# A two-layer decoder trunk on one core: which engine makes the low parts of the weights, and three smaller edits

## The chip, the cores and the metric

The kernel runs on one core of one Trainium2 chip. The metric is the device time of one execution in microseconds, as the median of several runs. TensorE (PE in the profile) multiplies, VectorE (DVE), ScalarE (ACT) and GpSimd (POOL) compute elementwise, SyncE (SP) issues most of the transfers.

## The reference

The input is one sequence of 256 tokens with 1024 features, all in float32. With `rms(x, g)` for x / sqrt(mean(x²) + 1e-6) · g:

```python
# layer 0
x = x + mlstm_layer(x, ...)      # rms -> q, k, v, o, gates; matrix memory in 4 heads; @ w_out
x = x + conv_ffn(x, layer 0)     # rms -> @ w_up (1024 x 5632), causal convolution of width 3,
                                 # silu(gate) * val, @ w_down (2816 x 1024)
# layer 1
k_sh, v_sh = rms(x, kv_norm_g) @ w_kv            # 3 dilation groups x 16 heads x 64
q = rms(x, b_norm_g) @ b_w_q
x = x + merge(dilated attention of 3 groups, relative bias) @ b_w_out
x = x + conv_ffn(x, layer 1)
return rms(x, final_norm_g)
```

## The kernel before

Features lie on the partitions: X is 128 x 8 x 256 (feature block k, token). Every weight matrix is read in **units** of 1024 x 256 float32 (1 MB), 124 in all, one after the other: 0 to 11 for the mLSTM's projections, 12 to 15 for its output, 16 to 37 for the first FFN up, 38 to 49 down, 50 to 85 for Q, K and V, 86 to 89 for the attention's output, 90 to 111 and 112 to 123 for the second FFN. Unit n lives in **slot** n % 3 of a ring of three (RING): `raw[s]` as loaded by SyncE's queue, `whi[s]` its high part, `wlo[s]` the low part. ScalarE makes the high part (`hi`, L487: a copy to fp32r). The low part is raw - whi, in `lo`: on VectorE (L832) two instructions of 128 x 1024, on GpSimd (L448) four of 128 x 512. Before the change VectorE does slot 0 and GpSimd slots 1 and 2 (unit 1 is shared). TensorE does three matmuls for each pair of k and column half: high · high, high · low (L1284, L1285), low · high (L1286). Activations are split likewise into `xsA`, `xsB`, `hs`, `aTs`.

Each engine runs its own hand-written order. `hi(n)` waits for the load and for TensorE to have used unit n - 3 (`w_used`). `lo(n)` waits for `hi_done`, TensorE for `lo_done` (in two halves), and the load of unit n + 3 for `lo_done` as well. Everything that stands behind a wait in an engine's order waits too.

- **mLSTM** (units 0 to 11). In pass u VectorE first calls `lo(u + 2)` and then does the work of gates and heads: `head_done` (L930 max, L933 reciprocal, L936 product), `head_normed` (L944, L946), and in pass 11 `gated` for k = 0 to 3 (L872) and `m_lo` (L878), on which the output projection waits.
- **Output projections** (`outproj`). VectorE adds each tile to X (`residual`, L897), ScalarE scales the new X (`gained`, L495) and squares it, VectorE makes the low part of the scaled X (`gained`, L848) and sums the squares (L857).
- **FFN up** (`ffn`, `pair`). A pair is two units, four tiles j in banks FB = (2, 3, 0, 1). VectorE scales a tile by rstd (`scaled`, L1069), ScalarE makes the first tap (`first_tap`, L664), VectorE the two others (`taps`, L1075 and L1079), and TensorE may use the bank again when the last tap is done (`cB_done`). VectorE calls `lo(n + 2)` at the start of the pair and `lo(n + 3)` behind the taps of tile 0. In the first pair `rstd_of` (L883, a reciprocal) is behind `lo(n + 2)`.
- **Attention** (`block`, four of them with nine units each). Tiles of Q, K and V are evacuated by `evac` (L1244, L1249, L1252); scores go into banks 3 to 5, a reduction with the bias gives the row maxima (L1169), ScalarE takes exp (L727) and normalises (L735), TensorE transposes (`turned`, L1551), ScalarE and VectorE split the transposed P (`p_hi` L751, `p_lo` L1187), and `mixed` multiplies P by V (L1570) into banks PV_BANK = (5, 4). In `mixed(0)` TensorE waits for `smax_done` of all eight score tiles, as scores use bank 5. In the last block the tiles of the output projection's first unit (`projected`) are interleaved with this.
- **End.** The sum of squares of the last norm (L1629, L1631), root (L519), reciprocal (L883). Then VectorE makes Y = X · gain · rstd for k = 0 to 4 (L1274), while GpSimd multiplies the three others, which ScalarE has scaled (L816), by rstd (L472). Four stores follow.

## Time and profile before

| | |
|---|---|
| median of 3 runs | 805.54 us (804.18 to 806.45) |
| the profiled execution | 804.01 us |
| its span, first to last instruction | 802.0 us |
| mean granted TensorE clock | 0.988 |
| TensorE busy | 768.8 us, 96% of the span |
| VectorE busy | 469.2 us |
| ScalarE busy | 458.9 us |
| GpSimd busy | 432.3 us |

Times in the trace are microseconds from the first instruction. The profiled execution is one of its own, 2 us longer than its span. A busy TensorE is not a TensorE at its peak, since matmuls overlap; the count of matmuls in a stretch and the granted clock tell more.

### The profile page before, as it was taken

What the parts mean: (1) busy time and instruction counts of PE and PEld (TensorE: products, weight loads), DVE (VectorE), ACT (ScalarE), POOL (GpSimd) and SP (SyncE); (2) the same over time, 40 slices, a digit from 0 to 9 for tenths busy, and PEclk for the clock granted to TensorE, in tenths of its full rate; (3) what the DMA queues carried; (4) which work ended last, traced back from release to release, by engine and by line L of the source; (5) the groups of instructions that cost most, each with busy time, mean ns of one, the idle gap of its engine ahead of it and who ended that gap; (6) DMA issues with size and microseconds to landing.
All of it is one profiled execution on the core that took longest, in us unless ns stands there. A gap on an engine that the chain in (4) does not pass through costs nothing.

```text
span 802.0 us, 17242 instructions
## 1 busy us (share of the span) xinstructions
PE 768.8 (96%) x6550; PEld 753.5 (94%) x6550; DVE 469.2 (58%) x905; ACT 458.9 (57%) x603; POOL 432.3 (54%) x346
## 2 busy tenths in 40 slices
PE   7999989999999999989999999999899999999994
PEld 6989989999999999989999999999899999999994
DVE  5766858767677344446435544635557767676333
ACT  6543547665666456358647737746756665665441
POOL 2843446666556667652563554452255666556851
PEclk9999989999999999999999999999999999999997
DMA  9634425646565456864676486476415756554721
GB/s 293 199 114 149 159 94 169 206 163 209 185 198 181 158 188 200 226 225 94 177 228 144 143 210 143 145 209 186 117 53 161 248 171 207 180 194 138 232 96 52
DMA packets 135612, 137.26 MB, mean 171 GB/s; under 512 B 3521, under 2 KB 134932, under 8 KB 135572
## 3 DMA queue, kind: packets, MB, share of 16 engines
q1 hardware_dynamic: 127808, 130.03, 49.8%
q10 hardware_dynamic: 7764, 6.67, 6.4%
q8 instruction: 28, 0.46, 0.2%
q14 instruction: 12, 0.10, 0.0%
HBM read 135.57 MB, written 1.12 MB: 170 GB/s over the span
## 4 chain that ended last, share of the span: by engine, by line
PE 77%; DVE 10%; ACT 5%; issue 4%; DMA 3%; DVEq 0%; ACTq 0%; SPq 0%
PE bank L1284 12%; PE bank L1286 12%; PE bank L1285 12%; PE banks L1284 8%; PE banks L1286 8%; PE banks L1285 8%; PE bank L1504 3%; PE banks L1570 3%; PE bank L1506 3%; PE bank L1505 3%; PE banks L1536 2%; PE banks L1551 2%; DVE wlo L832 2%; DMA raw<-in_w_kv 2%; ACT whi L487 2%
## 5 line engine op out<-in xcount | busy, mean ns | idle before, releaser
L448 POOL TENSOR_TENSOR wlo<-raw,whi 128x512 fp32r<-128x512 f32 (+1 forms) x325 | 423.4, 1337 | 335.0 <-ACT whi L487 334.8
L487 ACT ACTIVATE whi<-raw 128x2048 fp32r<-128x2048 f32 (+1 forms) x136 | 238.0, 1751 | 206.7 <-PE bank L1286 97.4
L1284 PE MATMUL bank<-xsA,whi 128*128 128x256 f32 x568 | 158.7, 279 | 6.7 <-DVE wlo L907 3.0
L1286 PE MATMUL bank<-xsA,wlo 128*128 128x256 f32 x568 | 157.0, 276 | 0.0
L1285 PE MATMUL bank<-xsA,whi 128*128 128x256 f32 x568 | 156.9, 276 | 0.0
L1284 PE MATMUL bank<-xsB,whi 128*128 128x256 f32 x480 | 134.3, 280 | 0.8 <-DVE X L897 0.3
L1286 PE MATMUL bank<-xsB,wlo 128*128 128x256 f32 x480 | 132.7, 276 | 0.0
L1285 PE MATMUL bank<-xsB,whi 128*128 128x256 f32 x480 | 132.6, 276 | 0.0
L832 DVE TENSOR_TENSOR wlo<-raw,whi 128x1024 fp32r<-128x1024 f32 x83 | 106.2, 1316 | 18.7 <-ACT whi L487 18.2
L1284 PEld LDWEIGHTS bank<-xsA,whi 128*128 128x128 f32 x568 | 106.6, 188 | 8.2 <-issue 3.8
L1285 PEld LDWEIGHTS bank<-xsA,whi 128*128 128x128 f32 x568 | 106.7, 188 | 0.1
L1286 PEld LDWEIGHTS bank<-xsA,wlo 128*128 128x128 f32 x568 | 106.6, 188 | 0.0
L1284 PE MATMUL banks<-hs,whi 128*128 128x256 f32 x352 | 97.2, 276 | 0.0
L1285 PE MATMUL banks<-hs,whi 128*128 128x256 f32 x352 | 97.2, 276 | 0.0
L1286 PE MATMUL banks<-hs,wlo 128*128 128x256 f32 x352 | 97.2, 276 | 0.0
L1284 PEld LDWEIGHTS bank<-xsB,whi 128*128 128x128 f32 x480 | 90.1, 188 | 2.8 <-DVE Vs L1252 1.0
L1285 PEld LDWEIGHTS bank<-xsB,whi 128*128 128x128 f32 x480 | 90.2, 188 | 0.0
L1286 PEld LDWEIGHTS bank<-xsB,wlo 128*128 128x128 f32 x480 | 90.1, 188 | 0.0
L1284 PEld LDWEIGHTS banks<-hs,whi 128*128 128x128 f32 x352 | 66.1, 188 | 0.0
L1285 PEld LDWEIGHTS banks<-hs,whi 128*128 128x128 f32 x352 | 66.1, 188 | 0.0
L1286 PEld LDWEIGHTS banks<-hs,wlo 128*128 128x128 f32 x352 | 66.1, 188 | 0.0
L1075 DVE SCALAR_TENSOR_TENSOR cb<-bank,vcols,cb 128x255 f32<-128x255 f32 x66 | 31.6, 479 | 51.4 <-ACT cb L664 51.2
(200 smaller groups left out, 1630.4 us busy)
## 6 DMA issues: line engine op xcount, KB each, us to landing
raw<-in_f_w_up SPq DMA_DIRECT2D x44, 1024.0 KB, 5.1
raw<-in_w_kv SPq DMA_DIRECT2D x24, 1024.0 KB, 5.4
raw<-in_f_w_down SPq DMA_DIRECT2D x16, 1024.0 KB, 5.2
raw<-in_b_w_q SPq DMA_DIRECT2D x12, 1024.0 KB, 5.2
raw<-in_a_w_in SPq DMA_DIRECT2D x10, 1024.0 KB, 5.6
raw<-in_f_w_down SPq DMA_DIRECT2D x8, 768.0 KB, 4.9
Bi<-bias_by_distance ACTq DMA_DIRECT2D x16, 384.0 KB, 6.2
raw<-in_a_w_out SPq DMA_DIRECT2D x4, 1024.0 KB, 5.3
```

The costliest lines, as they stand in the source:

```text
L448: o = g.tensor_tensor(wlo[s][:, ka:kb, :], raw[s][:, ka * CW:kb * CW] .rearrange("p (k c) -> p k c", c=CW), whi[s][:, ka:kb, :].bitcast(F3 ...
L487: o = a.activation(whi[s][:, k0:k1, :], raw[s][:, k0 * CW:k1 * CW] .rearrange("p (k c) -> p k c", c=CW), ACT.Copy)
L832: v.tensor_tensor(wlo[0][:, ka:kb, :], raw[0][:, ka * CW:kb * CW].rearrange("p (k c) -> p k c", c=CW), whi[0][:, ka:kb, :].bitcast(F32), A ...
L1075: v.scalar_tensor_tensor(cb[:, j, 1:S], bank[FB[j]][:, 0:S - 1], conv_col(layer, 1, p * 2 + (KF * g + c)), cb[:, j, 1:S], ALU.mult, ALU.ad ...
L1284: t_.matmul(ps, hi_w, hi_x, start=first, stop=False)
L1285: t_.matmul(ps, hi_w, lo_x, start=False, stop=False)
L1286: return t_.matmul(ps, lo_w, hi_x, start=False, stop=last)
L1504: t_.matmul(ps, xs[:, k, 0, cs], whi[s][:, k, :], start=first, stop=False)
L1505: t_.matmul(ps, xs[:, k, 0, cs], wlo[s][:, k, :], start=False, stop=False)
L1506: mm = t_.matmul(ps, xs[:, k, 1, cs], whi[s][:, k, :], start=False, stop=last)
L1536: mm = t_.matmul(score_out(2 * t + j)[:, g * w:(g + 1) * w], QT[rows, g, hp, tt * P:(tt + 1) * P], KT[rows, g, hp, 0:w], start=True, stop= ...
L1570: mm = t_.matmul(pv_out(h, slice(0, P))[:, kt * P:S], w, x[:, h, g, 2 * kt:2 + kt, :].rearrange("p b q -> p (b q)"), start=g == kt == 0 an ...
```

## The change

1. VectorE makes the low parts of slots 0 and 1, GpSimd those of slot 2 and of unit 18 (POOL_UNIT). In GpSimd's order: the rest of unit 1, then 2, 5, 8, 11, 14, 17, 18, 20, 23 and so on.
2. In the first FFN pair `rstd_of` comes before `lo(n + 2)`. In the attention block `evac(j, 0)` comes before `lo(n0 + j + 2)`; `lo(n0 + 9)` is called before `evac(8, 0)`; in the output projection `lo(u0 + 5)` is called in pass 2.
3. In the last block P times V of heads 0 and 1 goes to bank 2 instead of bank 5. `mixed(0)` then has no wait for `smax_done`, and the output projection waits for the low parts of these heads (`alo_done`) before its second unit, which uses bank 2.
4. For k = 0 to 4 of the last norm ScalarE writes X · gain into PSUM (`final_gained`, banks 0 to 2) during the last columns, and VectorE multiplies it by rstd with a tensor_tensor.

```diff
+POOL_UNIT = U_UP0 + 2
-PV_BANK = (5, 4)
+PV_BANK = ((5, 4), (2, 4))
...
-            return bank[PV_BANK[h // 2]][rows, (h % 2) * S:(h % 2 + 1) * S]
+            return bank[PV_BANK[last][h // 2]][rows, (h % 2) * S:(h % 2 + 1) * S]
...
+        def final_gained(k):
+
+            return bank[k // 2][:, k % 2 * S:(k % 2 + 1) * S]
# GpSimd
-            for n in range(U_IN, 6):
-                if n % RING:
-                    lo(n, k0=SHARE if n == 1 else 0)
+            lo(1, k0=SHARE)
+            lo(2)
+            lo(5)
...
-            with pool.Fori(0, (U_END - 7) // RING) as i:
-                for n in (7, 8):
-                    lo(n, i, RING)
+            with pool.Fori(0, (POOL_UNIT - 8) // RING + 1) as i:
+                lo(8, i, RING)
+            lo(POOL_UNIT)
+            with pool.Fori(0, (U_END - POOL_UNIT) // RING) as i:
+                lo(POOL_UNIT + 2, i, RING)
# ScalarE, ffn
                 warm_root()
+                if not sets:
+                    for k in range(Y_POOL):
+                        act.wait_ge(x_new, q0 + k + (1 - KD))
+                        a.activation(final_gained(k), X[:, k, :], ACT.Copy, scale=col(V_FIN + k))\
+                            .then_inc(yx_done, 1)
# VectorE, lo
-                if n % RING or n >= U_END:
+                s = n % RING
+                if s == 2 or n >= U_END or n == POOL_UNIT:
                     return
-                dve.wait_ge(hi_done[0], rnd(n, i, step) + 1)
+                dve.wait_ge(hi_done[s], rnd(n, i, step) + 1)
...
# VectorE, outproj
                     if u == 1:
                         lo(u0 + 3)
                         lo(u0 + 4)
+                    if u == 2:
+                        lo(u0 + 5)
# VectorE, pair
-                    lo(n + 2, i, step)
                     if first:
                         rstd_of(s, S)
+                    lo(n + 2, i, step)
                     scaled(p, 0, n, i, step)
# VectorE, block
                 for j in range(4):
+                    evac(j, 0)
                     lo(n0 + j + 2, i, step)
-                    evac(j, 0)
                     evac(j, 1)
...
                 a_lo(0)
                 a_lo(1)
+                lo(n0 + 9, i, step)
                 evac(8, 0)
# VectorE, end
+            dve.wait_ge(yx_done, Y_POOL)
             for k in range(Y_POOL):
-                v.scalar_tensor_tensor(Y[:, k, :], X[:, k, :], col(V_FIN + k), rstd[:, 0:S],
-                                       ALU.mult, ALU.mult).then_inc(yn_done, 1)
+                v.tensor_tensor(Y[:, k, :], final_gained(k), rstd[:, 0:S], ALU.mult)\
+                    .then_inc(yn_done, 1)
# TensorE, outproj
                 pe.wait_ge(ev_done, e0)
+                if begun:
+                    pe.wait_ge(alo_done, HB * (NHB - 1) + 2)
# TensorE, mixed
-                        pe.wait_ge(smax_done, hb * 8 + 8)
+                        if not last:
+                            pe.wait_ge(smax_done, hb * 8 + 8)
```

## Rows read from the trace of the kernel before

**Rows 1.** The page's first part: busy time, share, instructions of each engine.
```profile
PE 768.8 (96%) x6550; PEld 753.5 (94%) x6550; DVE 469.2 (58%) x905; ACT 458.9 (57%) x603; POOL 432.3 (54%) x346
```

**Rows 2.** Windows: stretch, its length, busy time and (instructions), clock, DMA share, GB/s.
```profile
105.00:110.00 5.00, 4.92 (x23) 4.95 (x24) 4.83 (x13) 2.85 (x8) 0.00 (x0) 0.50 0.63 210
351.00:356.00 5.00, 4.76 (x45) 4.64 (x46) 2.36 (x11) 2.70 (x7) 4.38 (x4) 1.00 1.04 340
575.00:578.00 3.00, 3.00 (x15) 3.00 (x16) 1.05 (x1) 0.98 (x2) 0.00 (x0) 0.50 0.20 49
160.00:260.00 100.00, 100.00 (x883) 100.00 (x883) 71.31 (x141) 61.43 (x74) 62.66 (x51) 1.00 0.58 189
```

**Rows 3.** Waits of TensorE: us in total, times, longest.
```profile
PE banks L1284 <- DVE xsB L878: 3.6, 1, 3.6
...
PE banks L1570 <- DVE mxx L1169: 2.4, 1, 2.4
PE banks L1536 <- DVE KT L1249: 2.3, 1, 2.3
```

**Rows 4.** L832: ns min/median/max; timeline of VectorE in the second output projection.
```profile
L832 DVE TENSOR_TENSOR wlo<-raw,whi x83: 1210/1219/2316, 11.6 to 779.2; 128x1024 fp32r<-128x1024 f32 x83
...
602.89 1.51 DVE L848 SCALAR_TENSOR_TENSOR xsB<-X,vcols,xsB 128x256 fp32r<-128x256 f32 x1
...
610.55 0.48 DVE L848 SCALAR_TENSOR_TENSOR xsB<-X,vcols,xsB 128x256 fp32r<-128x256 f32 x1 [0.32 <-ACT xsB L495]
```

**Rows 5.** Timeline of VectorE in the mLSTM: start us, us, instructions, [idle before].
```profile
75.73 1.35 DVE L930 TENSOR_TENSOR den<-den,EB 128x256 f32<-128x256 f32 x1 [2.38 <-ACT den L607]
...
98.46 1.50 DVE L946 TENSOR_TENSOR hm<-hm,hrs 128x512 f32<-128x512 f32 x1
...
100.22 4.38 DVE L872 SCALAR_TENSOR_TENSOR hm<-hm,vcols,sig 128x256 f32<-128x256 f32 x4
...
106.53 0.86 DVE L872 SCALAR_TENSOR_TENSOR hm<-hm,vcols,sig 128x256 f32<-128x256 f32 x2
```

**Rows 6.** Timeline of VectorE and ScalarE before the first FFN pair.
```profile
138.24 2.36 DVE L832 TENSOR_TENSOR wlo<-raw,whi 128x1024 fp32r<-128x1024 f32 x2 [1.88 <-ACT whi L487]
...
138.04 0.46 ACT L519 ACTIVATE rstd<-banks,epsc 128x256 f32<-128x256 f32 x1
```

**Rows 7.** Timeline of VectorE and ScalarE in the first attention block.
```profile
346.25 4.27 DVE L832 TENSOR_TENSOR wlo<-raw,whi 128x1024 fp32r<-128x1024 f32 x2 [3.74 <-ACT whi L487]
...
344.30 1.92 ACT L487 ACTIVATE whi<-raw 128x2048 fp32r<-128x2048 f32 x1 [0.96 <-DMA raw<-in_w_kv]
```

**Rows 8.** Timeline of TensorE and ScalarE in the last attention block.
```profile
574.88 0.48 PE L1570 MATMUL banks<-PTh,Vs 128*128 128x256 f32 x1 [2.44 <-DVE mxx L1169]
...
574.03 0.92 ACT L735 ACTIVATE SB<-SB,linv 128x768 f32<-128x768 f32 x1
...
581.08 0.94 ACT L735 ACTIVATE SB<-SB,linv 128x768 f32<-128x768 f32 x1
```

**Rows 9.** Timeline in the FFN pairs of layer 0; last, a wait in 160 to 268.
```profile
190.29 0.48 DVE L1079 SCALAR_TENSOR_TENSOR cb<-banks,vcols,cb 128x254 f32<-128x254 f32 x1
...
190.88 0.33 PE L1284 MATMUL banks<-xsA,whi 128*128 128x256 f32 x1
...
204.80 1.92 ACT L487 ACTIVATE whi<-raw 128x2048 fp32r<-128x2048 f32 x1 [2.10 <-PE banks L1286]
...
207.64 0.47 DVE L1075 SCALAR_TENSOR_TENSOR cb<-bank,vcols,cb 128x255 f32<-128x255 f32 x1
...
DVE cb L1075 <- ACT cb L664: 22.2, 12, 2.0
```

**Rows 10.** Timeline of VectorE, SyncE's queue and ScalarE at the end.
```profile
794.38 3.56 DVE L1274 SCALAR_TENSOR_TENSOR Y<-X,vcols,rstd 128x256 f32<-128x256 f32 x5
...
796.31 3.01 SPq L415 DMA_DIRECT2D out<-Y  x4
...
788.46 0.39 ACT L500 ACTIVATE banks<-X 128x256 f32<-128x256 f32 x1 [8.88 <-DVE X L897]
```

More of the change, by code:

```diff
@@ L269, in build @@
         ahi_done, alo_done = sem("ahi_done"), sem("alo_done")
-        yg_done = sem("yg_done")
+        yg_done, yx_done = sem("yg_done"), sem("yx_done")
         yn_done, yp_done = sem("yn_done"), sem("yp_done")
@@ L299, in own_rows, with pv_out, head_out @@
             return slice((h % 2) * DH, (h % 2 + 1) * DH)
-        def pv_out(h, rows):
-            return bank[PV_BANK[h // 2]][rows, (h % 2) * S:(h % 2 + 1) * S]
-        def head_out(hb, h, part):
+        def pv_out(h, rows, last):
+            return bank[PV_BANK[last][h // 2]][rows, (h % 2) * S:(h % 2 + 1) * S]
+        def head_out(hb, h, part, last):
             rows = own_rows(h)
@@ L310, in head_out @@
                 .rearrange("p a (b t) -> p (a b) t", b=NT)
-            src = pv_out(h, rows).rearrange("p (b t) -> p b t", b=NT)[:, :, ::-1]
+            src = pv_out(h, rows, last).rearrange("p (b t) -> p b t", b=NT)[:, :, ::-1]
             return dst, src
@@ L760, in a_cross @@
                         act.wait_ge(asum_done, hb * HB + (h - 1))
-                    a.activation(cross[own_rows(h), :], pv_out(h, own_rows(h + 1)), ACT.Copy)\
+                    a.activation(cross[own_rows(h), :], pv_out(h, own_rows(h + 1), last), ACT.Copy)\
                         .then_inc(cross_done, 1)
@@ L766, in a_hi @@
                     act.wait_ge(asum_done, hb * HB + (h + 1))
-                    a.activation(*head_out(hb, h, 0), ACT.Copy).then_inc(ahi_done, 1)
+                    a.activation(*head_out(hb, h, 0, last), ACT.Copy).then_inc(ahi_done, 1)
                 act.wait_ge(bv_out, 16)
@@ L825, in lo @@
             def lo(n, i=0, step=0, k0=0, k1=KD):
-                if n % RING or n >= U_END:
+                s = n % RING
+                if s == 2 or n >= U_END or n == POOL_UNIT:
                     return
-                dve.wait_ge(hi_done[0], rnd(n, i, step) + 1)
+                dve.wait_ge(hi_done[s], rnd(n, i, step) + 1)
                 for ka in range(k0, k1, KD // 2):
                     kb = ka + KD // 2
-                    v.tensor_tensor(wlo[0][:, ka:kb, :],
-                                    raw[0][:, ka * CW:kb * CW].rearrange("p (k c) -> p k c", c=CW),
-                                    whi[0][:, ka:kb, :].bitcast(F32), ALU.subtract)\
-                        .then_inc(lo_done[0], 1 if n else 2)
+                    v.tensor_tensor(wlo[s][:, ka:kb, :],
+                                    raw[s][:, ka * CW:kb * CW].rearrange("p (k c) -> p k c", c=CW),
+                                    whi[s][:, ka:kb, :].bitcast(F32), ALU.subtract)\
+                        .then_inc(lo_done[s], 1 if n else 2)
             def acc_clear(q):
@@ L1195, in a_sum @@
                     dve.wait_ge(cross_done, hb * HB + (h // 2 * 2 + 2))
-                    ps = pv_out(h, own_rows(h))
+                    ps = pv_out(h, own_rows(h), last)
                     v.tensor_tensor(ps, ps, cross[own_rows(h), :], ALU.add).then_inc(asum_done, 1)
@@ L1201, in a_lo @@
                     dve.wait_ge(ahi_done, hb * HB + (h + 1))
-                    dst, src = head_out(hb, h, 1)
-                    v.tensor_tensor(dst, src, head_out(hb, h, 0)[0].bitcast(F32), ALU.subtract)\
+                    dst, src = head_out(hb, h, 1, last)
+                    v.tensor_tensor(dst, src, head_out(hb, h, 0, last)[0].bitcast(F32), ALU.subtract)\
                         .then_inc(alo_done, 1)
                 for j in range(4):
+                    evac(j, 0)
                     lo(n0 + j + 2, i, step)
-                    evac(j, 0)
                     evac(j, 1)
@@ L1570, in mixed @@
                                     mm = t_.matmul(
-                                        pv_out(h, slice(0, P))[:, kt * P:S], w,
+                                        pv_out(h, slice(0, P), last)[:, kt * P:S], w,
                                         x[:, h, g, 2 * kt:2 + kt, :].rearrange("p b q -> p (b q)"),
```

## The prediction

> **What bounds the kernel now.** I read the page first: TensorE is busy for 96% of the span, VectorE for 58%, GpSimd for 54% [rows 1]. So no engine but TensorE can be worth more than TensorE's idle time. The table of windows shows that in the long FFN stretch TensorE runs 883 matmuls in 100 us with no idle time at the full 2.4 GHz [rows 2]; less work on GpSimd gains nothing there. The gain has to come from the few stalls between stages, so the waits of TensorE come next: 3.6 us for the low parts of the mLSTM output (L878), 2.4 us for the row maxima (L1169) in the last attention block, 2.3 us for a K tile (L1249) at the first block [rows 3]. After the longest two TensorE also runs at 1.2 GHz for a while, and after the 2.3 us stall it does not [rows 2]. Outside TensorE there is the tail after its last matmul. I then followed the timeline around each of these.
>
> **Who does the low parts.** There are 124 weight units. VectorE now splits the 41 whole ones of slot 0 (83 instructions of 1.22 us, L832, with one half [rows 4]). Afterwards GpSimd has slot 2 and unit 18, VectorE the rest of slots 0 and 1: 161 instructions, 39 units more on balance. A unit is two instructions of 1.22 us, 2.3 to 2.4 us; that is some 90 us more on VectorE and about 200 us less on GpSimd. Alone this is neither gain nor loss. What counts is where the 2.35 us lands, and what happens when both engines work at once: a scalar_tensor_tensor on operands in SBUF takes 0.48 us with GpSimd idle and 1.51 us while GpSimd subtracts [rows 4]. By the Trainium skill ("SBUF — State Buffer", Who interferes with whom) a VectorE instruction with two SBUF inputs contends with a GpSimd instruction that reads SBUF, and one of them waits for all of the other; these rows agree. The change takes most such overlaps away. The steps, in order of time:
>
> **mLSTM, to 105 us.** The chain here runs over VectorE. It now holds the splits of units 4, 7, 10 and 13. Unit 4 falls into slack. Unit 7 waits for ScalarE's copy and delays the gate exponents, estimated 0.3 us on TensorE. Unit 10 (2.35 us) cannot begin before 75.5 and precedes den at 75.73; den loses its contention (1.35 to 0.43 us) [rows 5]: about 1.1 us late. Unit 13 comes before the four hm products: 2.35 us added, but those four took 4.38 us against 0.86 for two without GpSimd [rows 5], so 2.7 us come back, and 0.8 us on L946 (1.50, of which I put 0.7 to its work). Sum 0.3 + 1.1 + 2.35 - 2.7 - 0.8: 0.3 us late. Bounds: 1 us gained to 2 lost. I take 0.4 lost. TensorE reaches this stall about 1.4 us later, so it idles about 2.5 us instead of 3.6. Whether the clock then falls I can't tell: idle 2.3 us it stayed up, idle 2.4 us (before L1570) it fell. The low clock cost 23 matmuls in 5 us where 44 fit [rows 2], about 2.5 us with its end. I take the fall as likelier.
>
> **First FFN pair, both layers.** In layer 0 the reciprocal of the root now precedes the split that sat in front of it (2.36 us at 138.24 [rows 6]), and that split goes to GpSimd; but the root is ready only at 138.5 [rows 6], and VectorE then gets unit 19 between the taps of the first tile and those of the second, while GpSimd is on unit 18. Of 2 us saved I keep 0.5 (0 to 2).
>
> **First attention block.** The K tile waits because the split of unit 57 (4.27 us, contended, begun at 346.25 when ScalarE had copied a slab that landed at 344.3) precedes both of its evacuations [rows 7]. Now the first of them goes ahead, and the other still waits for the split. The load of that slab is issued after unit 54's split as before; earlier loads go out 2 us sooner, but the bias loads hold the DMA engines then. If nothing but the first evacuation moves it gains 0.3 us, if the slab comes 2 us sooner all 2.3. I take 0.9. In the steady blocks the moved splits fit between softmax steps; two weight loads are issued together just before the bias loads, which may cost up to 2 us in one block: I take 0.2 lost.
>
> **Last attention block.** P times V of heads 0 and 1 starts at 574.88 after 2.44 us of idle time, because scores lie in bank 5 until their maxima are taken [rows 8]. With bank 2, whose last V tile VectorE has read before, it begins at 572.3 at full clock. The 16 matmuls before the transposes (some 3.4 us at the low clock, 15 in 3 us [rows 2]) then take 1.8; the transposes need ScalarE's normed P of 574.03 + 0.92 [rows 8], so TensorE idles 0.9 us. The next transposes need the copy at 581.08 [rows 8], which hangs on the former by way of p_hi, p_lo and inverse: it comes at 577.9, and all behind it by 3.2 us earlier. The new wait on alo_done stands before matmuls that TensorE reaches 2 us after it is met. Gain 3.2 us (2.0 if the transposes' chain takes 1.2 us back; 3.7 with the stall and the slow clock wholly gone).
>
> **Second output projection and its FFN pair.** The split of unit 91 leaves GpSimd for VectorE. The four STTs beside it took up to 1.51 us, and take 0.48 without it [rows 4]: some 3.3 us for the four, of which the new split takes 2.3 and waits for ScalarE 0.3. Net 0.7 us (0 to 1.5).
>
> **FFN pairs, 22 of them.** Three pairs last 32.6 us; VectorE is busy for 71.31% [rows 2], 23.3 us. Two more splits make 28.0. So it holds on average. But order matters: in a pair with a split behind its first taps, the second taps end at 190.77 and TensorE overwrites that bank at 190.88, with 0.33 us for a matmul that else lasts 0.28 [rows 9]: no slack. Where the preceding pair ended in a split, the first taps start 0.33 us later than they can (207.64, after 204.80 for the copy, against 2.51 us elsewhere [rows 9]). In the new pattern of slots these two meet every third pair, six times in both layers: 6 x 0.33, and with the smaller ones 2.0 us lost (0.5 to 5).
>
> **Tail.** Five STTs on X and rstd, both in SBUF, take 3.56 us beside GpSimd's three [rows 10]. With gained X in PSUM each has one SBUF input. At the pace of the pair that takes 0.86 us [rows 5] five take 2.0; a tensor_tensor is a little shorter, so I take 1.8. ScalarE's five copies come after the last table load, in 8.88 us in which it only waits for X [rows 10], and cost nothing; without that cover they would take 2 us. The four stores, issued over 3.01 us from 796.31 [rows 10], follow. Gain 1.8 us (1.2 to 2.2).
>
> **Sum.** Against the profiled execution's 804.01 us (span 802.0): gains 0.5 + 0.9 + 3.2 + 0.7 + 1.8 = 7.1; losses 0.4 + 0.2 + 2.0 = 2.6; net 4.5 us, 799.5. That execution lies 1.5 us under the median, 805.54; so 801.0 us.
>
> **Rivals.**
> 1. *The clock stays up at 105 us*, or the FFN pairs lose nothing. Each is worth 2 to 2.5 us: 798.5, with both 796.5. For it: 2.3 us idle left the clock alone [rows 2, 3]. Against it: 2.44 us brought it down in the last block [rows 2, 8].
> 2. *The move pays for itself and no more.* The FFN loss reaches its bound of 5 us and the last block gives 2: net 0.3, 805.2. That is no change.
> 3. *Slower: VectorE can't fill its waits in the FFN pairs.* Besides its busy time it waits 22.2 us in ten pairs for ScalarE's first tap (L664) [rows 9], 6.7 in three pairs. If no split fits into those, 28.0 + 6.7 = 34.7 us against 32.6: 2.1 us in each three pairs, 15 us in all, net 8.5 slower, 814. It is decided at 1.2 us for each three pairs (8.9 in all): above that the kernel is over 2.4 us slower. Against it: behind a split the first taps start 2.84 us after the copy, 0.33 late [rows 9], so that the split has filled the wait but for this. What would bring it about is contention: a split beside GpSimd took 4.27 us instead of 2.35 [rows 4, 7], and two such in three pairs add 3.8 us. VectorE's splits begin 3.6 and 9.0 us after the copy of a pair, when GpSimd, which starts as soon as its own slab is copied and needs 5.1 us, is done with slot 2 or has not begun, so I don't expect it. The Trainium skill ("Perfetto Trace Analysis", Optimizing Scalar/DVE Operations) says that moving work between these two engines might not help, as they share a port; the rows that bear it out are those of the contended split.
>
> **Chances.** Forecast, 799 to 803: 0.50. Rival 1, 796 to 799: 0.27. Rival 2, 803 to 808: 0.15. Rival 3: 0.08. The measurement can tell 0.3%, 2.4 us. Faster than 803.1: 0.79; within: 0.14; slower than 808: 0.07. Both ends of the range, 796.5 and 804.3, take in rival 1 and half of rival 2.
>
> **What would show it.** L832 x161, L448 x169, the latter never beside L872. L1570's first start in the last block within 0.3 us of the matmul before, at full clock. The five products at the end within 2 us. Waits of TensorE for L1079 in every third pair, 0.3 us each; if they are 1.2 us or in every pair, rival 3. At the first block the wait for L1249 shorter than 2.0 us. The granted clock between 104 and 111 us tells rival 1. The prediction fails if the FFN stretch runs under 870 matmuls in 100 us, or if the last block's chain gives less than 2 us.

## The result, and the profile after

The changed kernel takes 797.8 us in the median (795.02 to 799.05, five runs) and the kernel before 804.18 us (803.63 to 806.45) beside it. By the medians that is 6.4 us faster. The ratio of the two is put at 0.9899, 95% interval 0.9881 to 0.9917, which is 8.1 us (6.7 to 9.6); the same pair measured again (experiment 5) gives 7.1 us by the medians and 7.2 by the ratio. The profiled execution took 795.02 us with a span of 793.0, 9.0 us under the span of before. One of all the runs in this document, in experiment 4, was a slow one of 865.7 us at a mean granted clock of 0.843; the ratio and the range there leave it out. Three parts of the prediction's sum came out to 0.1 us, and the total still fell short of the measured change, so the places matter more than the total.

The page's first part and two of its groups. GpSimd has 190 instructions instead of 346 [rows 1], VectorE 161 instructions of its split, two to a unit, instead of 83 [rows 4].

```profile
PE 767.4 (97%) x6550; PEld 751.1 (95%) x6550; DVE 538.5 (68%) x983; ACT 462.4 (58%) x608; POOL 226.7 (29%) x190
...
L453 POOL TENSOR_TENSOR wlo<-raw,whi 128x512 fp32r<-128x512 f32 (+1 forms) x169 | 218.2, 1324 | 530.4 <-ACT whi L494 530.4
...
L845 DVE TENSOR_TENSOR wlo<-raw,whi 128x1024 fp32r<-128x1024 f32 x161 | 197.9, 1267 | 15.8 <-ACT whi L494 15.1
```

Waits of TensorE in the changed kernel, to be held against [rows 3]: the mLSTM's wait (xsB, L891) has shrunk from 3.6 to 2.3 us, and those for the row maxima and for KT are gone. Of the seven waits for cb (L1094) in the first line two are old: 1.24 and 1.18 us in the first pair of either layer, where before waited 1.49 and 1.22. The other five, 0.15 to 0.16 us each, are new, and a sixth is too short for the list.

```profile
PE banks L1301 <- DVE cb L1094: 3.2, 7, 1.2
PE banks L1301 <- DVE xsB L891: 2.3, 1, 2.3
...
PE banks L1570 <- ACT SB L747: 1.3, 2, 0.7
...
PE banks L1590 <- DVE PTl L1202: 0.5, 1, 0.5
```

Windows of the changed kernel (columns as in [rows 2]): behind the mLSTM's stall, in the FFN pairs of either layer, and the P times V of the last block. Where before ran 23 matmuls at a clock of 0.50 this execution runs 42 at 1.00; the FFN pairs have lost their full house, 872 and 869 matmuls where 883 and 881 fitted; and nothing in the last block is at the low clock.

```profile
105.00:110.00 5.00, 5.00 (x42) 4.85 (x43) 4.82 (x14) 2.98 (x7) 0.00 (x0) 1.00 0.48 169
155.00:255.00 100.00, 99.54 (x872) 98.95 (x871) 83.76 (x153) 62.10 (x74) 30.35 (x24) 1.00 0.59 190
...
632.00:732.00 100.00, 99.53 (x869) 98.85 (x868) 82.76 (x150) 60.91 (x72) 30.35 (x24) 1.00 0.55 183
...
568.00:571.00 3.00, 2.29 (x21) 2.15 (x20) 2.62 (x8) 3.00 (x6) 0.00 (x0) 1.00 0.00 2
```

The two traces have the same 6550 matmuls, so the plainest comparison is when a matmul of a given number starts in each. The table is that start minus the start in before's profiled execution; two executions of the changed kernel, the split alone (experiment 1) and before with the end alone (experiment 3) stand side by side. The last runs before's code up to the last matmuls, so that it shows how far before's own profiled execution can be taken as usual.

| behind (matmul, its time in before) | changed, 793.0 us | changed again, 795.3 us | split alone, 799.2 us | end alone, 800.6 us | predicted |
|---|---|---|---|---|---|
| mLSTM's stall and clock (760, 111.5) | -2.6 | -1.2 | -1.25 | -1.15 | +0.4 |
| first FFN pair (1060, 149.3) | -3.5 | -1.2 | -1.2 | -1.2 | -0.1 |
| FFN pairs of layer 0 (2700, 336.0) | -2.2 | +0.1 | 0.0 | -1.3 | +0.9 |
| first attention block (3300, 407.7) | -4.5 | -2.15 | -2.3 | +0.4 | 0.0 |
| the other blocks (4600, 558.1) | -4.5 | -2.1 | -1.8 | +0.4 | +0.2 |
| last block (4740, 578.8) | -7.7 | -5.3 | -3.3 | +0.5 | -3.0 |
| second output projection (5000, 611.6) | -8.5 | -6.1 | -4.1 | +0.5 | -3.7 |
| FFN pairs of layer 1 (5860, 712.0) | -7.15 | -4.9 | -2.8 | +0.4 | -2.7 |
| end | -9.0 | -6.7 | -2.85 | -1.4 | -4.5 |

Read the second column against the first: the same kernel, 2.3 us apart, all of it gained before matmul 1060 and nothing after. The experiments below had to say what that is. And read the fourth column by itself: before's code, run again, is 1.2 us ahead of before's profiled execution behind the mLSTM and loses 1.7 us against it in the first block. Experiments 2 and 4 do the like (2.5 and 1.2 us ahead, then 2.1 and 1.95 lost), and this changes what the stages of the change are worth.

### The profile page after: what moved, and what is told of

The parts are those of the page before. It is cut to its first block, busy times and chain, and to the rows that moved or that the text cites. A ratio compares the mean times of both kernels' runs of the same rounds, so it can differ in the third digit from the quotient of the medians.

```text
span 793.0 us, 17171 instructions
## 1 busy us (share of the span) xinstructions
PE 767.4 (97%) x6550; PEld 751.1 (95%) x6550; DVE 538.5 (68%) x983; ACT 462.4 (58%) x608; POOL 226.7 (29%) x190
## 4 chain that ended last, share of the span: by engine, by line
PE 53%; DVE 24%; issue 11%; ACT 7%; DMA 2%; DVEq 1%; ACTq 0%; POOL 0%; POOLq 0%
DVE wlo L845 9%; PE bank L1301 7%; PE bank L1303 6%; PE bank L1302 6%; PE banks L1301 6%; PE banks L1303 6%; PE banks L1302 6%; DVE cb L1090 3%; PE bank L1523 3%; PE banks L1590 2%; PE bank L1525 2%; DVE bank L1084 2%; ACT cb L671 2%; PE bank L1524 2%; PE banks L1555 2%
## 5 line engine op out<-in xcount | busy, mean ns | idle before, releaser
L453 POOL TENSOR_TENSOR wlo<-raw,whi 128x512 fp32r<-128x512 f32 (+1 forms) x169 | 218.2, 1324 | 530.4 <-ACT whi L494 530.4
L845 DVE TENSOR_TENSOR wlo<-raw,whi 128x1024 fp32r<-128x1024 f32 x161 | 197.9, 1267 | 15.8 <-ACT whi L494 15.1
L1523 PE MATMUL bank<-whi,xsA 128*128 128x256 f32 x192 | 56.8, 296 | 0.0
```

What stands on the lines that cost most here:

```text
L453: o = g.tensor_tensor(wlo[s][:, ka:kb, :], raw[s][:, ka * CW:kb * CW] .rearrange("p (k c) -> p k c", c=CW), whi[s][:, ka:kb, :].bitcast(F3 ...
L845: v.tensor_tensor(wlo[s][:, ka:kb, :], raw[s][:, ka * CW:kb * CW].rearrange("p (k c) -> p k c", c=CW), whi[s][:, ka:kb, :].bitcast(F32), A ...
L1523: t_.matmul(ps, xs[:, k, 0, cs], whi[s][:, k, :], start=first, stop=False)
```

## The experiments

Each group of experiments has runs of before beside it: 804.93 us median for the first four, 804.49 for the next four, 805.03 for 9 to 11 and 804.58 for 12. Differences are of medians within a group, where nothing else is said.

**1. The split alone.** The changed kernel without its points 3 and 4:

```diff
-PV_BANK = ((5, 4), (2, 4))
+PV_BANK = ((5, 4), (5, 4))
...
-                        if not last:
-                            pe.wait_ge(smax_done, hb * 8 + 8)
+                        pe.wait_ge(smax_done, hb * 8 + 8)
...
-            dve.wait_ge(yx_done, Y_POOL)
...
-                v.tensor_tensor(Y[:, k, :], final_gained(k), rstd[:, 0:S], ALU.mult)\
-                    .then_inc(yn_done, 1)
+                v.scalar_tensor_tensor(Y[:, k, :], X[:, k, :], col(V_FIN + k), rstd[:, 0:S],
+                                       ALU.mult, ALU.mult).then_inc(yn_done, 1)
```

> The changed kernel with the old banks for P times V and the old end: only the move of slot 1's low parts to VectorE and the new places of the splits. My theory: the move alone gains 3.5 to 4 us in the profiled execution: 2.7 by 105 us if the clock stays at 2.4 GHz there (0.2 if it falls), 0.5 in the first FFN pair, 2.3 in the first attention block, 0.7 in the second output projection, less 2.6 in the FFN pairs (six waits for L1094's counterpart of 0.3 us, and smaller ones). The rival, that the move only pays for itself and the gain is all in the bank and the end, expects a total within 1 us of the kernel before.

802.33 us (800.4 to 805.11), ratio 0.9974 [0.996, 0.9987]: 2.6 us faster, the span 2.85 shorter, with the clock fallen at 105 us. That is neither the theory's 3.5 to 4 nor the rival's "within 1 us". The wait for KT is gone with this part alone, and the 2.44 us for the maxima stand. The table shows 1.5 us gained in the last block all the same: behind that unchanged stall the clock was 1.00 (39 matmuls from 575 to 580 us), in before's execution 0.66 (31). It fell in experiments 3, 4 and 9 as well, so this part of the gain is not shown to be the split's.

**2. Bank 2 alone** (before with point 3) and **3. the end alone** (before with point 4):

```diff
# 2
-PV_BANK = (5, 4)
+PV_BANK = ((5, 4), (2, 4))
...
+                if begun:
+                    pe.wait_ge(alo_done, HB * (NHB - 1) + 2)
...
-                        pe.wait_ge(smax_done, hb * 8 + 8)
+                        if not last:
+                            pe.wait_ge(smax_done, hb * 8 + 8)
# 3, with ScalarE's five products of point 4
...
+            dve.wait_ge(yx_done, Y_POOL)
             for k in range(Y_POOL):
-                v.scalar_tensor_tensor(Y[:, k, :], X[:, k, :], col(V_FIN + k), rstd[:, 0:S],
-                                       ALU.mult, ALU.mult).then_inc(yn_done, 1)
+                v.tensor_tensor(Y[:, k, :], final_gained(k), rstd[:, 0:S], ALU.mult)\
+                    .then_inc(yn_done, 1)
```

> The kernel before with bank 2 for P times V of heads 0 and 1 in the last block, its wait for the maxima gone and the new wait in the output projection; nothing else. My theory: 3.2 us faster, TensorE's 2.4 us wait before L1570's line gone, no stretch at 1.2 GHz near 575 us, and a wait of 0.7 to 0.9 us for the transposes in its place. The rival, that the chain of transposes takes it back, expects 2.0 us or less.

> The kernel before with the gained X of the last norm in PSUM; nothing else. My theory: VectorE's five products take 1.8 us instead of 3.56, and the span is 1.8 us shorter from the last matmul on. The rival, that the stores or GpSimd's three products decide the end, expects under 0.5 us. ScalarE's five copies should start within the stretch in which it waits for X, and no other wait should grow.

Bank 2: 801.29 us, ratio 0.996 [0.9947, 0.9973]. Between matmuls 4600 and 4740 its trace gains 3.25 us, the predicted 3.2. In the place of the wait for L1169 stands the one that the prediction had named, ScalarE's normed P, and it is short. TensorE's timeline there, and then VectorE's at the end of the kernel with the end alone:

```profile
574.50 0.88 PE L1560 MATMUL banks<-ident,SB 128*128 128x128 f32 x6 [0.78 <-ACT SB L740]
```
```profile
794.83 1.75 DVE L1287 TENSOR_TENSOR Y<-bank,rstd 128x256 f32<-128x256 f32 x5
```

The end: 802.28 us, ratio 0.9972 [0.996, 0.9984]; behind the last matmul its trace gains 1.8 us, five products in 1.75 us instead of 3.56 [rows 10].

Both kernels run before's code up to the first attention block, and both lose there what before's profiled execution did not. The wait for KT is 3.0 and 2.5 us instead of 2.3, and behind it the clock falls, while in [rows 2] it stood at 1.00 with 45 matmuls in 5 us. Against before, experiment 2 loses 2.1 us between matmuls 2700 and 3300 and experiment 3 loses 1.7. Windows of 2 and of 3, then their waits:

```profile
350.00:355.00 5.00, 5.00 (x39) 4.78 (x38) 2.17 (x10) 2.29 (x6) 3.44 (x3) 0.75 1.09 363
```
```profile
350.00:355.00 5.00, 4.84 (x32) 4.62 (x33) 2.02 (x11) 1.44 (x4) 4.27 (x4) 0.66 1.05 347
```
```profile
PE banks L1545 <- DVE KT L1256: 3.0, 1, 3.0
```
```profile
PE banks L1549 <- DVE KT L1261: 2.5, 1, 2.5
```

**4. The order alone** (before with the two moves of point 2: the root ahead of the split, the first evacuation ahead of the split).

```diff
-                    lo(n + 2, i, step)
                     if first:
                         rstd_of(s, S)
+                    lo(n + 2, i, step)
...
+                    evac(j, 0)
                     lo(n0 + j + 2, i, step)
-                    evac(j, 0)
```

> The kernel before with the two new places alone: the reciprocal before the split in the first FFN pair, and the first evacuation before the split in the attention blocks. GpSimd keeps slot 1. If the order is what removed the wait in the first attention block, TensorE's 2.3 us wait for L1249's counterpart goes here too and the kernel is some 2 us faster. My theory: it is the weight slab, which now lands 2 us sooner, and the contention; the order alone gives 0.3 us, and the wait stays at about 2 us.

807.66 us (805.59 to 808.61, nine runs), ratio 1.0029 [1.0016, 1.0043]: slower. VectorE's and TensorE's timelines at the first FFN pair: the root, ready at 137.3, now goes first, the split follows and takes 3.46 us, and both stand between TensorE and its evacuation.

```profile
137.34 1.75 DVE L889 RECIPROCAL rstd<-rstd 128x256 f32<-128x256 f32 x1 [2.24 <-ACT rstd L524]
139.13 3.46 DVE L838 TENSOR_TENSOR wlo<-raw,whi 128x1024 fp32r<-128x1024 f32 x2
142.51 0.42 DVE L1075 TENSOR_TENSOR bank<-bank,rstd 128x256 f32<-128x256 f32 x1
```
```profile
144.61 0.39 PE L1291 MATMUL bank<-xsA,whi 128*128 128x256 f32 x1 [2.90 <-DVE cb L1085]
```

Before, the split filled the time in which VectorE waited for the root. Behind this longer wait the clock fell too (33 matmuls from 145 to 150 us at 0.66, where before's execution has 46 at 1.00), so the trace loses 3.0 us in this stage. In the changed kernel the split at that place is GpSimd's, and there the move costs nothing (experiment 7). Nor did it shorten the first block's wait, which stood at 2.8 us, with a loss of 1.95 us against before's execution there.

**5. The changed kernel again**, as the control of the next three.

> The changed kernel again, unedited, as the control for the three kernels beside it. Its time should repeat: 797.8 us median before, 795 to 799. Theory A (the step down to the low clock behind the stall near 101 us is a matter of phase, as the kernels with parts of the change show: with the same gap of 3.61 us in two of them one had 30 matmuls in the 5 us from 105 us on at a granted clock of 0.69, another 42 at 1.00): the profiled execution may show this window at 1.00 or below it, and its span goes with that, 793 to 796. Theory B (the shorter gap of 2.33 us is what keeps the clock up): 42 matmuls at 1.00 again.

797.35 us (796.21 to 799.1), ratio 0.991 [0.9893, 0.9928]. This time the clock fell. The window from 105 to 110 us in five executions, in this order: changed again, bank 2 alone, the end alone, the order alone, the split alone.

```profile
105.00:110.00 5.00, 5.00 (x30) 5.00 (x31) 4.83 (x14) 2.96 (x7) 0.00 (x0) 0.66 0.49 171
```
```profile
105.00:110.00 5.00, 4.99 (x42) 4.86 (x43) 4.82 (x14) 2.88 (x7) 0.00 (x0) 1.00 0.64 207
```
```profile
105.00:110.00 5.00, 4.76 (x30) 4.79 (x31) 4.83 (x14) 2.86 (x8) 0.00 (x0) 0.69 0.61 210
```
```profile
105.00:110.00 5.00, 4.97 (x30) 5.00 (x31) 4.82 (x14) 2.86 (x8) 0.00 (x0) 0.69 0.64 209
```
```profile
105.00:110.00 5.00, 4.96 (x31) 4.99 (x32) 4.82 (x14) 2.85 (x8) 0.00 (x0) 0.69 0.53 181
```

The middle three are before's code up to there, with a stall of 3.61 us in each; in one the clock stayed up, in two it came down. The first and the last had 2.3 us, as the first execution of the changed kernel, where it stayed up, as it did in experiment 8. So the length of the stall does not decide it, and theory A holds as far as that; what does decide it is not shown. The traces have one mark of it. In the three executions that kept the clock at 105 us (changed, experiments 2 and 8) it had been low from 11 to 14 us (0.50, 0.53, 0.55); in the seven others it stood at 1.00 there. Both are found with before's code (0.53 in experiment 2; 1.00 in before, 3 and 4), so that the executions differ from their start. The clock also explains only 1.4 of the 2.3 us between the two executions of the changed kernel. The rest goes with a stall at 128 us, with VectorE's and GpSimd's timelines of the second execution, and then those of the first:

```profile
125.48 1.52 DVE L861 SCALAR_TENSOR_TENSOR xsA<-X,vcols,xsA 128x256 fp32r<-128x256 f32 x1
...
127.26 1.18 DVE L861 SCALAR_TENSOR_TENSOR xsA<-X,vcols,xsA 128x256 fp32r<-128x256 f32 x1
...
125.21 5.62 POOL L453 TENSOR_TENSOR wlo<-raw,whi 128x512 fp32r<-128x512 f32 x4 [8.90 <-ACT whi L494]
...
129.25 0.36 PE L1301 MATMUL bank<-xsA,whi 128*128 128x256 f32 x1 [0.71 <-DVE X L910]
```
```profile
124.12 0.47 DVE L861 SCALAR_TENSOR_TENSOR xsA<-X,vcols,xsA 128x256 fp32r<-128x256 f32 x1
...
124.85 0.47 DVE L861 SCALAR_TENSOR_TENSOR xsA<-X,vcols,xsA 128x256 fp32r<-128x256 f32 x1
...
124.97 5.65 POOL L453 TENSOR_TENSOR wlo<-raw,whi 128x512 fp32r<-128x512 f32 x4 [8.66 <-ACT whi L494]
```

VectorE's two steps are all but done when GpSimd's split begins in one execution (the second ends at 125.32, the split begins at 124.97) and fall under it in the other: 0.9 us or 2.7 us for the two.

**6. The split behind the taps** in the FFN pairs:

```diff
                     taps(p, 0)
-                    lo(n + 3, i, step)
                     if not first:
                         h_lo(p - 1)
                     scaled(p, 2, n, i, step)
                     taps(p, 1)
+                    lo(n + 3, i, step)
```

> The changed kernel with one edit: in the feed-forward pairs VectorE makes the low part of unit n+3 behind the taps of row 1, not ahead of them. Theory A (the low part sits between the scaling of one row and the taps that TensorE's bank waits for, so that it sets both the steady stalls, six of 0.43 us from start to start in the profiled execution, and part of the first pairs' stalls of 1.24 and 1.18 us): 2 to 4.5 us faster than the changed kernel, about 794. Theory B (the low part is then late for TensorE's own correction matmuls, or the next bank waits instead): within 0.5 us of it or slower, the same six gaps with another releaser.

792.59 us (789.64 to 793.6), ratio 0.9836 [0.9815, 0.9857]: 4.8 us under experiment 5 by the medians, 4.3 by the traces, both of which have the fall of the clock. The windows show 884 and 885 matmuls in 100 us: the six steady stalls are gone, and those of 1.28 and 1.18 us in the first pairs too. By the starts of the matmuls, against the control: 1.6 and 1.5 us at the two first pairs, 1.1 and 0.4 us in the pairs behind them, where a new wait of 0.7 us at 622 us takes back some of layer 1's.

```profile
155.00:255.00 100.00, 100.00 (x884) 100.00 (x884) 85.23 (x155) 62.82 (x76) 32.11 (x24) 1.00 0.58 187
...
632.00:732.00 100.00, 100.00 (x885) 100.00 (x884) 84.43 (x151) 60.01 (x71) 31.36 (x24) 1.00 0.56 182
```

**7. The changed kernel in the old order** (the diff of 4 reversed).

> The changed kernel with the old places of the two edits of order: the root ahead of the low part in the first pair, and the first evacuation ahead of the low part in the attention blocks. Theory A (in the changed kernel the unit that the first pair would split at that place is not VectorE's, so the root's place is free; and in the blocks VectorE is idle long enough): within 0.5 us of the changed kernel. Theory B (the order carries the first block's gain of 2.3 us): the wait of TensorE for KT near 345 us comes back with 1 to 3 us.

798.27 us (796.6 to 802.69), ratio 0.9932 [0.9908, 0.9956], 0.9 us above the control with ranges that overlap; its trace is 0.47 us longer than the control's. The two waits for KT are 0.3 us each, and 2.1 us are gained in the first block against the control's 2.3. Theory A: the order does not carry the first block.

**8. Unit 52 back on GpSimd.**

```diff
# GpSimd, between its units 50 and 53
+            lo(U_QKV + 2)
...
# VectorE, lo
-                if s == 2 or n >= U_END or n == POOL_UNIT:
+                if s == 2 or n >= U_END or n in (POOL_UNIT, U_QKV + 2):
```

> The changed kernel with the low part of unit 52 alone back on GpSimd. Theory A (the wait of TensorE in the first attention block was for the slab of unit 57, whose load is issued once the low part of the unit in its buffer three before has been made, so that a faster split two units back pulls the whole chain of loads forward by about 2 us): the slabs of units 56 and 57 land 1 to 2 us later against TensorE's own progress, and a wait for KT of 1 to 2 us comes back; time 1 to 2 us above the changed kernel. Theory B (what removed the wait is VectorE's own shorter work at the block, not the loads): no wait for KT, time within 0.5 us.

801.63 us (797.85 to 808.26), ratio 0.9977 [0.9956, 0.9998], 4.3 us above the control; one unit out of 80. ScalarE's and VectorE's timelines with it, TensorE's wait, and then ScalarE's and VectorE's of the changed kernel:

```profile
341.27 1.92 ACT L497 ACTIVATE whi<-raw 128x2048 fp32r<-128x2048 f32 x1 [0.87 <-DMA raw<-in_w_kv]
...
343.23 4.37 DVE L848 TENSOR_TENSOR wlo<-raw,whi 128x1024 fp32r<-128x1024 f32 x2 [0.97 <-ACT whi L497]
...
347.99 0.94 PE L1558 MATMUL banks<-KT,QT 64*128 64x128 f32 x12 [2.06 <-DVE KT L1268]
```
```profile
340.07 1.92 ACT L494 ACTIVATE whi<-raw 128x2048 fp32r<-128x2048 f32 x1 [1.03 <-DMA raw<-in_w_kv]
...
342.94 3.44 DVE L845 TENSOR_TENSOR wlo<-raw,whi 128x1024 fp32r<-128x1024 f32 x2
```

The slab lands 1.2 us later by the clock of the trace while TensorE is 0.8 us ahead: 2.0 us, with its own load issued at the same time against TensorE's progress (325.72 and 328.37 us for the two loads, 328.37 + 0.76 = 329.13 as in the changed kernel). What differs is the load before it, which goes out 2.0 us later and still fills the queue. The wait for KT is back with 2.06 us, and in this execution the clock fell behind it (0.74 from 350 to 355 us), another 1.4 us. Theory A, and dearer than it said: 3.5 us at the block by the trace. The profiled execution is the fastest of the twelve and had the clock up at 105 us, so it is only 0.8 us longer than the control's; what spreads the other runs up to 808.26 us was not traced.

**9 to 11. Matmuls into the stall.** Ahead of the first output projection, in before (14), in the changed kernel (8) and in the kernel of 6 (8):

```diff
+            pe.wait_ge(den_abs, 4)
+            for _ in range(FILL):
+                t_.matmul(bank[7][:, 0:P], ones[:], ones[:], start=True, stop=True)
             outproj(U_AOUT, E_UP0, xsB, lambda k: pe.wait_ge(mlo_done, k + 1), 8, OB0, False)
```

> The kernel before, with 14 matmuls of ones by ones into bank 7 in the stall of 3.6 us ahead of the first output projection; nothing reads what they write. They leave the stall's end where it is, if TensorE waits for xsB and not for them. Theory A (what TensorE loses behind that stall is the step down to 1.2 GHz: 23 matmuls at a granted clock of 0.50 from 105 to 110 us in the profiled execution of before, 42 at 1.00 in another execution of the same code there): the window shows over 40 matmuls at 1.00 in every execution, and the time is 1.2 to 2.6 us below before's. Theory B (the engine's records only show the low clock, and the next wait, for xsA near 131 us, ends when it ended before): no more than 0.3 us.

> The changed kernel with 8 such matmuls in its stall of 2.33 us at the same place. The two profiled executions of the changed kernel differ by 2.3 us, all of it behind this stall: 1.2 us by 15 matmuls at half the clock and 1.1 us by a stall of 0.71 us at 128 us, where VectorE's last steps of the norm (1.52 and 1.18 us beside GpSimd's low part, 0.47 us each where they end ahead of it) come late. Theory A (both follow from the step down): granted clock 1.00, no stall at 128 us, median 1 to 2.3 us below the changed kernel's 797.4, and less spread. Theory B (the phase is given by something else, the bias's or the weights' transfers): the median and the spread stay.

> The changed kernel with both edits, the low part of unit n+3 behind the taps of row 1 and the 8 matmuls in the stall. The first alone measured 792.6 us median, 789.6 to 793.6, with the step down in its profiled execution. Theory A (the two are independent): 789.5 to 791 us, at the lower end of the first one's runs. Theory B (the step down only moves to the next stall): 792.6 as before.

| | median, us | range | window 105 to 110 |
|---|---|---|---|
| before with 14 | 803.11 (1.9 under before) | 801.04 to 804.98 | 41 matmuls, 1.00 |
| changed with 8 | 796.93 (0.4 under experiment 5, of another group) | 796.34 to 797.94 | 42, 1.00 |
| kernel of 6 with 8 | 791.0 (1.6 under 6, of another group) | 790.59 to 791.32 | 42, 1.00 |

No profiled execution with the filler shows the fall. In before it was worth 1.9 us, 0.9974 [0.9962, 0.9986]: in its trace 2.5 us are gained up to the first block against before's profiled execution, 1.2 against experiment 3's. The 1.8 us that it loses in the first block are not the filler's, since experiments 2, 3 and 4 lose 1.7 to 2.1 there as well. In the changed kernel no gain is shown: the ratio is 0.9905 [0.989, 0.992] after 0.991 [0.9893, 0.9928] without. The clock held and the stall at 128 us remained, so theory A was right of the one half and wrong of the other. The traces of 10 and 11 also had the low clock near 11 us that marks the executions which held it without a filler; those of 9 and 12 had not, and held it all the same. GpSimd's slab had landed sooner, and its split fell on VectorE's two steps all the same:

```profile
123.93 5.62 POOL L454 TENSOR_TENSOR wlo<-raw,whi 128x512 fp32r<-128x512 f32 x4 [7.55 <-ACT whi L495]
...
124.21 1.52 DVE L862 SCALAR_TENSOR_TENSOR xsA<-X,vcols,xsA 128x256 fp32r<-128x256 f32 x1
...
127.97 0.36 PE L1302 MATMUL bank<-xsA,whi 128*128 128x256 f32 x1 [0.70 <-DVE X L911]
```

The third has the lowest time of this study: ratio 0.9828 [0.9812, 0.9845] to before, 14.0 us, about twice the gain of the change itself. That of experiment 6 is 0.9836 [0.9815, 0.9857], so the part of the eight matmuls in it is not shown beyond the 1.3 us by which its trace is ahead at matmul 760.

**12. The fifth unit's low part behind the third's residual**, in that kernel:

```diff
                     if u == 1:
                         lo(u0 + 3)
-                        lo(u0 + 4)
                     if u == 2:
+                        lo(u0 + 4)
                         lo(u0 + 5)
```

> The kernel with both edits (791.0 us median), and in the output projections the low part of the fifth unit behind the residual of the third, not ahead of it. In its profiled execution and in that of the changed kernel with the filler alone a stall of 0.70 us stood at 127 us: VectorE had two low parts in a row (4.62 us), then two last steps of the norm of 1.52 and 1.18 us beside GpSimd, which had its weights 1.3 us sooner than in the first profiled execution of the changed kernel, where the same steps took 0.47 us each and TensorE had no such stall. Theory A (the residual is late because both low parts stand ahead of it): the stall goes, 0.3 to 1 us faster. Theory B (the fifth unit's low part is now what is late): a stall of 0.3 to 1 us with the low part as its releaser, no gain.

792.42 us (791.22 to 793.02), ratio 0.9843 [0.9829, 0.9857]: 1.4 us slower than 11 by the medians and 1.5 by the traces, with intervals that overlap. The stall of 0.70 us is gone as theory A had it, the gain is not: the split now runs beside GpSimd, 4.48 us instead of 2.3, and two stalls for the steps behind it take its place. This is theory B with another releaser than it named.

```profile
124.23 4.48 DVE L846 TENSOR_TENSOR wlo<-raw,whi 128x1024 fp32r<-128x1024 f32 x2
...
131.62 0.39 PE L1302 MATMUL bank<-xsA,whi 128*128 128x256 f32 x1 [0.39 <-DVE xsA L862]
133.41 0.38 PE L1302 MATMUL bank<-xsA,whi 128*128 128x256 f32 x1 [0.82 <-DVE xsA L862]
```

## Why the prediction was wrong, and where it was right

The sign was right, and 797.8 us lies between the outer bounds, 796.5 and 804.3. But the forecast of 801.0, with 799 to 803 for its own band, missed; the time fell into rival 1's band, and largely for another reason than rival 1's. The change was put at 4.5 us and is 6.4 us by the medians of the first runs and 7.1 by those of the second. The step of 1.5 us from the profiled execution to the median did not hold either: beside the changed kernel before's median was 804.18 and not 805.54.

One reading runs through the sum: before's profiled execution was taken as what before's code does. The second execution of the changed kernel and experiment 3, both with the clock fallen at 105 us, give the change stage by stage. It gains under 0.1 us at the mLSTM, 4.0 in the first block, 3.2 in the last, 0.8 in the second output projection and 1.8 at the end (against before); it loses 0.1 in the first FFN pair and 2.6 in the FFN pairs. That makes 7.1 us, the difference of the medians. It is 2.6 us over the forecast: the first block alone brings 3.1, and the other terms together take 0.5 back.

**First attention block ("I take 0.9"): the step that failed.** Against before's profiled execution 2.3 us were gained in both executions and in experiment 1, and against experiments 2, 3 and 4 it is 4.0 to 4.4 us. Two things were wrong. The prediction had both ends, 0.3 and 2.3, and put its value near the lower, since the bias loads would hold the DMA engines. The load was long indeed (10.9 us from issue to landing), yet the slab landed 2.0 us sooner against TensorE's progress. Experiments 7 and 8 settle it: the order is not what does it, the earlier load is, and with unit 52 alone back on GpSimd the wait returns. What I had not followed is that a load gains by its predecessor's going out earlier even if its own issue does not move. And the prediction said that after the 2.3 us stall TensorE does not run at 1.2 GHz, from the one execution of before in which that is so. In experiments 2, 3, 4 and 9, which have this wait too, the clock fell behind it each time, and 1.7 to 2.1 us more were lost there. The change saves these with the wait, and no term had them.

**mLSTM, to 105 us ("I take 0.4 lost", "I take the fall as likelier"): nothing lost, and the clock hid it.** TensorE did come 1.1 us later to the stall (1.4 forecast), but idled 2.33 us instead of 2.5, and went on 0.2 us sooner than before. Like with like the change is worth almost nothing here. With the clock fallen the second execution stands 1.2 us ahead of before's, but so do experiments 3 and 4 with before's code (1.15 and 1.2). With the clock up the first stands 2.6 ahead and experiment 2, again before's code, 2.5. What looks like a gain is that before's profiled execution had the dearest fall of all: 25 matmuls started at the low clock's pace, 11 to 16 in the other six. I weighed one fall against one stall without a fall and made of it a rule about length, so that the step's price of 2.5 us would stay or go as a whole. It does neither. Of the ten executions without matmuls in the stall, the clock fell in seven and stayed up in three, at either length of stall. Rival 1 came true in the first execution and not in the second; it was no property of the kernel.

**First FFN pair (0.5 us):** 0.9 in the first execution, 0 in the second. The collision at 128 us, in neither term nor bound, makes the difference. The wait at the pair itself is 1.24 us after 1.49. A wait of 1.19 us for the low part of xsA (L848) at 135 us, which no term names, is gone in both, and new short ones have come.

**FFN pairs (2.0 lost):** 2.6 lost. The mechanism is as described, splits behind taps in every third pair, six places, but each costs 0.44 us by the starts of the matmuls, and not 0.33, since it is the last tap's end that TensorE waits for. VectorE's timeline at the first of the six in the changed kernel, where the split of 2.35 us stands ahead of the taps:

```profile
172.43 2.35 DVE L845 TENSOR_TENSOR wlo<-raw,whi 128x1024 fp32r<-128x1024 f32 x2
...
176.25 0.48 DVE L1094 SCALAR_TENSOR_TENSOR cb<-banks,vcols,cb 128x254 f32<-128x254 f32 x1
...
176.78 0.39 PE L1301 MATMUL banks<-xsA,whi 128*128 128x256 f32 x1 [0.16 <-DVE cb L1094]
```

Experiment 6 shows that it was the place and not the work: with the same splits on VectorE the loss in these pairs is nil. Rival 3 is out: 872 matmuls in 100 us of layer 0, just over the 870 that the prediction had set as its mark, though layer 1 has 869, just under it.

**Last block (3.2), second output projection (0.7), tail (1.8):** 3.2, 0.8 and 1.8. P times V starts at once behind the tiles before it and at full clock, the transposes wait 0.71 us for ScalarE (0.9 forecast), and the five products take 1.75 us with four stores issued in 2.35 behind them:

```profile
570.54 0.88 PE L1570 MATMUL banks<-ident,SB 128*128 128x128 f32 x6 [0.71 <-ACT SB L747]
```
```profile
787.24 1.75 DVE L1291 TENSOR_TENSOR Y<-bank,rstd 128x256 f32<-128x256 f32 x5
...
788.01 2.35 SPq L420 DMA_DIRECT2D out<-Y  x4
```

**The other blocks (0.2 lost):** nothing, but for a wait for KT in the third block in some executions (0.5 and 0.3 us by the starts in experiments 1 and 7).

What stays open is what tips the clock at a stall of given length, and what sets the load issued at 116.4 us, on which the collision at 128 us depends. It took 5.0 to 5.1 us in the seven executions in which the clock fell and 6.5 to 7.2 in the three in which it held, so one thing may lie behind both; with the filler, where the clock held, it took 5.1 to 5.2. The parts alone add up: by their ratios they are worth 2.1, 3.2 and 2.3 us, together 7.6, and the whole 8.1 and 7.2. By the medians it is 8.9 against 6.4 and 7.1, but each part's interval is 1.9 to 2.2 us wide.

## What to carry to other kernels

When work moves to an engine with spare time, look where in its order it lands: in this kernel the same splits ahead of one tile's taps cost 4.8 us more than behind them. Follow a freed engine to the transfers that it releases, and the transfer before the one that is waited for as well. And do not price a stall and the clock behind it from one profiled execution, of the kernel before above all: take the same window from several, or fill the stall and measure.

## What the runs showed of the hardware

- The clock behind a stall varies between executions of the same code: after 3.6 us idle 0.50, 0.69, 0.69 and 1.00 (105 to 110 us), after 2.33 us 1.00 twice and 0.66 to 0.69 four times; after 2.44 us in the last block 0.66 in before and experiments 3, 4 and 9 and 1.00 in experiment 1. In the first block it stayed at 1.00 after 2.34 us in before and fell after 2.06, 2.54, 2.63, 2.80 and 3.03 us in experiments 8, 3, 9, 4 and 2. Fourteen or eight 128x128 matmuls in the stall kept it at 1.00 in each of the four profiled executions that had them (two of which may have held it anyway, see experiments 5 and 10), and the spread of six runs of the changed kernel went from 2.9 to 1.6 us with them. The Trainium skill ("TensorE: Matmul & The Clock Gate", Part 1: The HAM clock gate) says that the check of the engine's activity is free-running and not tied to the kernel, so that the count of slow matmuls varies from run to run; these ten executions agree, with 0 or 11 to 25 of them behind one stall.
- A scalar_tensor_tensor of 128x256 took 0.47 us alone and 1.18 to 1.52 beside GpSimd's subtraction, and a VectorE split of two instructions 2.35 alone, 3.44, 4.37 and 4.48 beside it. GpSimd paid too: four of its instructions took 5.0 us alone and 7.18 beside VectorE's split in experiment 12. These rows agree on both sides with the rule that the prediction takes from the Trainium skill ("SBUF — State Buffer", Who interferes with whom): now the one engine waits, now the other.
